# Fifteen instead of nine paired projection parts in the first block, the convolution's four among them

## The chip, the cores and the metric

The kernel runs on one NeuronCore of one Trainium2 chip. TensorE multiplies matrices, VectorE (DVE) and ScalarE (ACT) work element by element, GpSimd (POOL) does little here, and SyncE (SP) issues the DMAs. The metric is the device time of one launch in microseconds: 2176.01 us, the median of three runs (2175.82 to 2176.3).

## The reference, cut to what matters

Two transformer blocks of two layers each follow one another, on 256 rows of 1024 values. The change touches only the first block, whose mixer begins with one wide projection. Its parts go to a state-space branch with a short convolution, and to three kinds of attention:

```python
def causal_dwconv(u, w, b):
    width = w.shape[0]                                    # 4 taps
    up = jnp.pad(u, ((0, 0), (width - 1, 0), (0, 0)))
    y = lax.conv_general_dilated(up, w[:, None, :], window_strides=(1,), padding='VALID',
                                 dimension_numbers=('NWC', 'WIO', 'NWC'),
                                 feature_group_count=u.shape[-1])
    return y + b

def hybrid_mixer(h, w_in, ...):
    u = h @ w_in                                          # [256, 1024] @ [1024, D_IN]
    (z, xs, bs, cs, dt_raw, fq, fk, fv, ff, mq, mk, mv, dq, dk, dv, iq, ik, iw) = jnp.split(
        u, np.cumsum(IN_SPLITS)[:-1].tolist(), axis=-1)
    y_ssm = mamba2_branch(z, xs, bs, cs, dt_raw, ...)      # silu(causal_dwconv(xs, bs, cs)), then a scan
    y_fox = fox_branch(fq, fk, fv, ff, fox_fbias)
    ...
```

The result must agree with float32 arithmetic, so every product is made of split operands: a weight w becomes whi + wlo and an activation x becomes nhi + nlo, and three products (whi nhi, whi nlo, wlo nhi) are summed.

## The kernel before

**Parts.** The weights come in parts of 1 MB, numbered h in the order in which TensorE wants them. Parts 0 to 3 are the lead (z and fv). Part 4 holds a few narrow columns. Parts 5 to 8 hold the 1024 channels of the convolution (256 channels each, two blocks of 128), part 9 the index queries, parts 10 and 11 fq, parts 12 and 13 fk, then the rest. For each part SyncE issues a DMA, ScalarE makes the high half (`hi`, L1161), VectorE the low half (`lo`, L1444), and TensorE multiplies.

**Two ways to multiply a part of 256 channels.** A plain part fills one PSUM bank: its block m = 0 goes to columns 0 to 255 and m = 1 to 256 to 511. `block_of` (L656) issues three matmuls of 256 columns for each of eight row blocks k, so 24 for a block of 128 channels. A paired part (list `PAIRED`) fills a bank for each block of 128 channels: `apart_block` multiplies whi once with nlo and nhi side by side (512 columns, L666, 8 matmuls), then wlo with nhi (256 columns, L670, 8 matmuls). The bank then holds two sums in two halves. ScalarE copies one to SBUF (`evict_half`, L1202) and VectorE adds the other to it (`add_half`, L1695).

**Banks.** Units of the projection alternate between banks 0 and 1. `bank(key)` makes TensorE wait until the unit two before has been freed:

```python
            u = unit[key]
            if u >= 2:
                pe.wait_ge(*freed[u - 2])
```

A plain unit is a whole part and is freed by ScalarE's copy (`free_a`). A paired unit is a half part and is freed by VectorE's addition (`pair_sum`).

**The order on each engine is written by hand,** one step i after another. VectorE in step i does: the addition of half 1 of part i-1, `lo(i + 2)`, the addition of half 0 of part i, and then what belongs to the step. That is two blocks of the convolution each in steps 6 to 9, the small softplus chain in 6 and 9 (`softplus_1` to `softplus_3`, L1536 to L1563), `cumulated` in 11, the rotations `rope(0)` and `rope(1)` in 12, and `state_inputs` in 13 (L1602, L1604). One block b of the convolution is one L1518 and three L1521, each waiting for the one before it. ScalarE in step i does: the copy of part i-1 (or of its half 1), `hi(i + 3)`, the copy of half 0 of part i, and then its own extras. In step 9 an `Ln` waits for VectorE's `softplus_2`, and in step 10 come two `Silu`, the first of which (L1325) waits for the whole convolution.

**Between the parts TensorE does** `cumulate` after part 10 (L830, L833), `state_scores` in the middle of part 12 (L841 to L847, ends with `xs_ps`), and `decay(0)` after two matmuls of part 14 (L857 and on). The last waits for `xs_ok`, which `state_inputs` gives.

SyncE swaps halves of the index queries for the rotation once part 9 has been freed.

Of the kernel before, what the change touches and what calls it, by code (L numbers as in the profile page):

```python
# [132 lines left out]
def earlier(n_first, n_second):  # L133
# [6 lines left out]
GAINED_1 = {  # L140
    "wk_ps": 18, "wk_free": 9, "qv_ps": 9,
    "gpost_in": 64, "par_in": 48, "small_in": 96, "sgw_in": 320,
    "w_small": 368, "tr_ps": 8, "full": 51, "half_used": 44, "par_ps": 1, "few_ps": 1, "cum_ps": 5, "cb_ps": 1,
    "xs_ps": 1, "dec_ps": 8, "ix_ps": 1, "y_ps": 1, "qk_ps": 12, "yt_ps": 4, "pt_ps": 6, "o_ps": 6, "pr_ps": 16,
    "out_used": 3, "mix_ps": 2, "dn_ps": 2, "in_ms": 4, "hi_ok": 87, "nhi_ok": 8, "free_a": 33, "spe": 21,
    "silu_ok": 2, "cb_ok": 1, "dec_ok": 8, "ix_rl": 1, "ex_ok": 12, "yt_out": 1, "pt_a": 6, "ot_ok": 6,
    "sig_ok": 4, "yh_ok": 4, "mh_ok": 4, "ssq_ok": 6, "ms_ok": 6, "fg_free": 11, "hh_ok": 11, "xn_ok": 8,
    "nlo_ok": 8, "lo_ok": 87, "pad_ok": 2, "par_ok": 1, "spv": 20, "lcat_ok": 5, "cum_ok": 2, "free_v": 10,
    "rope_ok": 10, "xs_ok": 1, "sc_ok": 2, "msq_ok": 1, "mx_ok": 12, "yt_ok": 1, "pn_ok": 12, "pt_v": 6,
    "isc_ok": 1, "pen_ok": 2, "yl_ok": 4, "pr_free": 16, "mg_ok": 14, "ml_ok": 4, "x_ok": 4, "fu_free": 11,  # L150
    "hs_ok": 11, "in_rs": 2, "rstd_ok": 7
}
GAINED_2 = {
# [51 lines left out]
FEW = [(0, 6416, 68), (68, 1516, 28), (96, 3056, 32)]  # L205
H_FEW, H_XBC = 4, 5
ROWS_1 = (19, 24)
PAIRED = (10, 11, 13, 14, 15, 16, 21, 22, 23)
C_IW, C_DT, C_FF = 64, 88, 120
N_GATE1 = 16  # L210
N_PARTS1 = N_IN1 + N_GATE1 + 12 + HID1 // 128 + KH1 // 2
# [26 lines left out]
def first_block(nc, ctx, sems, n_chain, ps, x, x_in, con, con_in, con_bf, bfc, start, a):  # L238
# [107 lines left out]
    hi_ok, lo_ok = sem("hi_ok"), sem("lo_ok")  # L346
    full, free_a, free_v = (sem(n) for n in ("full", "free_a", "free_v"))
    par_ps, par_ok = sem("par_ps"), sem("par_ok")
    ssq_ok, ms_ok, msq_ok, rstd_ok = sem("ssq_ok"), sem("ms_ok"), sem("msq_ok"), sem("rstd_ok")
# [7 lines left out]
    in_ms, in_rs = sem("in_ms"), sem("in_rs")  # L357
# [8 lines left out]
    fg_free, fu_free, hh_ok, hs_ok, dn_ps = (sem(n) for n in ("fg_free", "fu_free", "hh_ok", "hs_ok", "dn_ps"))  # L366
    sum_a, gate_sum, up_sum = sem("wk_ps"), sem("wk_free"), sem("qv_ps")
    dch = sem("dch")
    pair_half, pair_sum = spe, spv
    bias_in, biased, mg_turned = [small_in, swap_in[1]], lcat_ok, cum_ps  # L370
    BIAS_BEFORE = (64, 336)

# [47 lines left out]
    order = []  # L420
    order += [("lead", name, t) for _, name in LEAD for t in range(NT)]
    for i in range(4, N_IN1 + N_GATE1):
        order += [("in", i, n) for n in range(2 if i in PAIRED else 1)] if i < N_IN1 else [("gate", i - N_IN1)]
    unit = {key: u for u, key in enumerate(order)}
    pairs = {("in", i, n): 2 * PAIRED.index(i) + n + 1 for i in PAIRED for n in range(2)}
    freed = [(pair_sum, 2 + pairs[key]) if key in pairs else (free_a, n + 1 - sum(k in pairs for k in order[:n]))
             for n, key in enumerate(order)]
    filled = {key: n + 1 for n, key in enumerate(order)}

# [207 lines left out]
    def tensor(pe, l, prior, following):  # L637
# [384 lines left out]
        for n in range(4):  # L1022
            yhi, ylo = ybuf[n % 2]
            for m in range(4):
                h, t = H_BR + 2 * n + m // 2, m % 2
                i = 4 * n + m
                if m == 0:
                    pe.wait_ge(yl_ok, n + 1)
                if t == 0:
                    pe.wait_ge(lo_ok, h + 1)  # L1030
                if i == 15:
                    merged_turn(0)
                if i >= 4:
                    pe.wait_ge(pr_free, i - 3)
                hi, lo = high(l, h), low(l, h)
                for k in range(4):
                    for j, (x_, w) in enumerate(((ylo, hi), (yhi, lo), (yhi, hi))):
                        mm = T.matmul(ps[:, 4 + i % 4, :], x_[:, k, t * P:(t + 1) * P], w[:, k, :],  # L1038
                                      start=k == 0 and j == 0, stop=k == 3 and j == 2)
                mm.then_inc(pr_ps, 1)  # L1040
# [122 lines left out]
    def scalar(act, l, prior, following):  # L1163
# [133 lines left out]
        for i in range(1, H_BR):  # L1297
            if i <= 2:
                evict_lead(i - 1)
            if i == 4:  # L1300
                evict_lead(2)
                evict_lead(3)
            if i == 5:
                act.wait_ge(par_ok, 1)
            if 5 <= i <= N_IN1:
                if i - 1 == 22:
                    act.wait_ge(qk_ps, 4)
                if i - 1 in PAIRED:
                    evict_half(i - 1, 1)
                elif i - 1 not in ROWS_1:  # L1310
                    evict(i - 1)
            hi(i + 3)
            if i in PAIRED:
                if i == 22:
                    act.wait_ge(qk_ps, 4)
                evict_half(i, 0)
            if i > N_IN1:
                evict_gate(i - 1 - N_IN1)
            if i - 1 in ROWS_1:
                if i - 1 == ROWS_1[1]:  # L1320
                    act.wait_ge(o_ps, 2)
                evict(i - 1)
            if i == 10:
                act.wait_ge(pad_ok, 2)
                S.activation(xbc[:, :, :], xbc[:, :, :], ACT.Silu).then_inc(silu_ok, 1)  # L1325
                act.wait_ge(*freed[unit["lead", "z", 1]])
                S.activation(z[:, :, :], z[:, :, :], ACT.Silu).then_inc(silu_ok, 1)
            if i == 8:
                act.wait_ge(spv, 1)
                S.activation(sp[:, 2, :], sp[:, 1, :], ACT.Exp, scale=-1.0).then_inc(spe, 1)  # L1330
                act.wait_ge(small_in, 64)
                S.activation(asg[:, 0:8], small[:, 1, :], ACT.Exp).then_inc(spe, 1)
            if i == 9:
                act.wait_ge(spv, 2)
                S.activation(sp[:, 4, :], sp[:, 3, :], ACT.Ln).then_inc(spe, 1)
            if i == 13:
                act.wait_ge(cb_ps, 1)
                S.copy(cb[:, :, :], ps[:, 2:4, 0:384]).then_inc(cb_ok, 1)
            if i == 14:
                decays(0)  # L1340
            if i == 15:
                decays(1)
            if i == 17:
                relus()
            if i == 20:
                y_out()
            for n in range(6):
                if i == Q_STEP[n]:
                    exps(n, 0)
                if i == Q_STEP[n] + 1:  # L1350
                    exps(n, 1)
                if i == Q_STEP[n] + 2:
                    p_out(n)
                if i == Q_STEP[n] + 4:
                    o_out(n)
            if i == 37:
                branch_hi(0)
                sigmoids(0)
            if i == 38:
                branch_hi(1)  # L1360
            if i == 39:
                sigmoids(1)
            if i == 41:
                sigmoids(2)
# [113 lines left out]
    def vector(dve, l, prior, following):  # L1478
# [33 lines left out]

        def convolve(b):
            if b % 2 == 0:
                dve.wait_ge(*freed[unit["in", H_XBC + b // 2, 0]])
            dve.wait_ge(pad_ok, 1)
            dve.wait_ge(par_ok, 1)
            link(V.tensor_scalar(xbc[:, b, :], xbcp[:, b, 0:SEQ], parT[:, PCW + b:PCW + b + 1],  # L1518
                                 parT[:, PCB + b:PCB + b + 1], ALU.mult, ALU.add))
            for j in range(1, 4):  # L1520
                ins = V.scalar_tensor_tensor(xbc[:, b, :], xbcp[:, b, j:j + SEQ],  # L1521
                                             parT[:, PCW + 8 * j + b:PCW + 8 * j + b + 1],
                                             xbc[:, b, :], ALU.mult, ALU.add)
                if b == 7 and j == 3:
                    ins.then_inc(pad_ok, 1)
                else:
                    link(ins)
# [163 lines left out]
        def add_half(i, m):  # L1691
            _, _, _, name, at_ = IN1[i][2][0]
            out = dst[name][:, at_ + m, :]
            dve.wait_ge(pair_half, 3 + pairs["in", i, m])
            V.scalar_tensor_tensor(out, ps[:, unit["in", i, m] % 2, SEQ:2 * SEQ], QSCALE.get(name, 1.0), out,  # L1695
                                   ALU.mult, ALU.add).then_inc(pair_sum, 1)

# [6 lines left out]
        def gated(i):  # L1704
            n, m = i // 4, i % 4
            if m == 0:
                dve.wait_ge(sig_ok, n + 1)
            dve.wait_ge(pr_ps, i + 1)
            src = ps[:, 4 + i % 4, :]
            t, c = m % 2, 512 * (m // 2)  # L1710
            gt = gates_of(n)[:, t, c:c + 512]
            out = merged[:, t, c:c + 512]
            product = rt[:, :, :].rearrange("p a b -> p (a b)")
            if n == 0:
                V.tensor_tensor(out, src, gt, ALU.mult).then_inc(pr_free, 1)
                return
            if i > 4:
                dve.wait_ge(mg_ok, i - 4)
            V.tensor_tensor(product, src, gt, ALU.mult).then_inc(pr_free, 1)
            dve.wait_ge(pr_free, i + 1)  # L1720
            V.tensor_tensor(out, out, product, ALU.add).then_inc(mg_ok, 1)
# [2487 lines left out]
```

## Time and profile before

| | us |
|---|---|
| median of three runs | 2176.01 |
| the profiled execution | 2175.88 |
| its span, first to last instruction | 2174.0 |
| TensorE busy | 2157.4 (99%) |
| VectorE busy | 1487.8 (68%) |
| ScalarE busy | 1118.6 (51%) |

The span is cut into instructions for each engine. A row of the timeline has the start, the time to the end, the engine, the line, output and inputs, and in brackets how long the engine had been idle and who released it. Matmuls overlap, so the time that one costs is read from start to start. In the same way a VectorE instruction's successor starts some 0.08 us before its end. The first block's first layer has its projection from about 21 us on; the second layer repeats it 532.1 us later.

### The profile page before, as it was taken

To read this page: it belongs to the slowest core of one execution; us is meant where nothing else is said; L and a number is where in the kernel's file an instruction comes from. 1 tells how busy PE (TensorE), PEld (TensorE's weight loads), DVE (VectorE), ACT (ScalarE), POOL (GpSimd) and SP (SyncE) were. 2 spreads that over 40 slices of the span, in tenths; PEclk is the share of its full clock that TensorE was granted. 3 is DMA by queue.
4 is the path that set the end of the run, shared out by engine and by line. 5 is a ranking of instruction groups with operands and counts; after the bars stand their busy time and mean duration, and the time that the engine had idled before them with its cause. 6 is when DMAs were issued, how large, how long until landed. Compare 5 with 4: busy or idle time off the path is not lost.

```text
span 2174.0 us, 30972 instructions
## 1 busy us (share of the span) xinstructions
PE 2157.4 (99%) x13072; PEld 1852.7 (85%) x13072; DVE 1487.8 (68%) x1660; ACT 1118.6 (51%) x1413; POOL 44.7 (2%) x46
## 2 busy tenths in 40 slices
PE   8999999999999999999999999999999999999998
PEld 7988888888988888888898888988889888898887
DVE  6788677655778868666678777456557877745654
ACT  5555555454565564545466535444446653544442
POOL 0000000000000000000000100000000010000000
PEclk9999999999999999999999999999999999999999
DMA  8555564655664556556564444456566444545652
GB/s 278 167 167 176 168 232 160 208 197 168 198 186 155 162 204 203 177 190 214 161 197 135 143 150 162 150 170 192 191 171 204 134 143 151 160 151 169 193 192 76
DMA packets 248751, 380.75 MB, mean 175 GB/s; under 512 B 22495, under 2 KB 158693, under 8 KB 248614
## 3 DMA queue, kind: packets, MB, share of 16 engines
q1 hardware_dynamic: 248614, 378.78, 54.2%
q8 instruction: 103, 1.69, 0.3%
q14 instruction: 34, 0.28, 0.0%
HBM read 372.26 MB, written 1.05 MB: 172 GB/s over the span
## 4 chain that ended last, share of the span: by engine, by line
PE 97%; DVE 2%; ACT 1%; issue 1%; DMA 0%; POOL 0%; DVEq 0%; SPq 0%; POOLq 0%; ACTq 0%
PE ps L666 9%; PE ps L2567 8%; PE ps L803 8%; PE ps L3137 8%; PE ps L2471 7%; PE ps L2518 5%; PE ps L1135 5%; PE ps L2492 5%; PE ps L670 5%; PE ps L656 5%; PE ps L2625 4%; PE ps L1038 4%; PE ps L2494 2%; PE ps L762 2%; PE ps L1056 2%; PE ps L2588 2%
## 5 line engine op out<-in xcount | busy, mean ns | idle before, releaser
L3498 DVE TENSOR_TENSOR b_wlo<-b_ring,b_whi 128x2048 fp32r<-128x2048 f32 (+2 forms) x168 | 379.4, 2262 | 107.8 <-ACT b_whi L3162 107.1
L1444 DVE TENSOR_TENSOR a_wlo<-a_ring,a_whi 128x2048 fp32r<-128x2048 f32 (+1 forms) x173 | 392.8, 2273 | 56.9 <-ACT a_whi L1161 56.5
L3162 ACT CAST b_whi<-b_ring 128x2048 fp32r<-128x2048 f32 (+2 forms) x168 | 318.1, 1893 | 202.2 <-PE ps L3137 76.0
L1161 ACT CAST a_whi<-a_ring 128x2048 fp32r<-128x2048 f32 (+1 forms) x173 | 329.0, 1903 | 150.1 <-PE ps L1038 45.2
L666 PE MATMUL ps<-a_nsp,a_whi 128*128 128x512 f32 x864 | 218.4, 394 | 0.0
L666 PEld LDWEIGHTS ps<-a_nsp,a_whi 128*128 128x128 f32 x864 | 155.2, 189 | 27.9
L2567 PE MATMUL ps<-b_whi,b_nsp 128*128 128x512 f32 x512 | 170.9, 400 | 0.0
L803 PE MATMUL ps<-a_whi,a_nsp 128*128 128x512 f32 x512 | 162.3, 392 | 0.0
L670 PEld LDWEIGHTS ps<-a_nsp,a_wlo 128*128 128x128 f32 x864 | 117.8, 190 | 8.5
L670 PE MATMUL ps<-a_nsp,a_wlo 128*128 128x256 f32 x864 | 120.4, 282 | 0.0
L2567 PEld LDWEIGHTS ps<-b_whi,b_nsp 128*128 128x128 f32 x512 | 96.1, 188 | 20.9
L803 PEld LDWEIGHTS ps<-a_whi,a_nsp 128*128 128x128 f32 x512 | 96.1, 188 | 20.3 <-issue 0.3
L2492 PE MATMUL ps<-b_nsp,b_whi 128*128 128x512 f32 x448 | 112.5, 393 | 0.0
L2567 PE MATMUL ps<-b_wlo,b_nsp 128*128 128x512 f32 x256 | 99.9, 390 | 0.0
L3137 PE MATMUL ps<-b_whi,b_hlo 128*128 128x512 f32 x256 | 99.8, 390 | 0.0
L803 PE MATMUL ps<-a_wlo,a_nsp 128*128 128x512 f32 x256 | 99.7, 389 | 0.0
L3137 PE MATMUL ps<-b_wlo,b_hhi 128*128 128x512 f32 x256 | 99.6, 389 | 0.0
L3137 PE MATMUL ps<-b_whi,b_hhi 128*128 128x512 f32 x256 | 99.6, 389 | 0.0
L2471 PE MATMUL ps<-b_nsp,b_whi 128*128 128x256 f32 x544 | 98.5, 283 | 0.0
L656 PE MATMUL ps<-a_nsp,a_whi 128*128 128x256 f32 x544 | 98.4, 283 | 0.0
L2492 PEld LDWEIGHTS ps<-b_nsp,b_whi 128*128 128x128 f32 x448 | 80.6, 189 | 14.5
L2471 PEld LDWEIGHTS ps<-b_nsp,b_whi 128*128 128x128 f32 x544 | 84.8, 192 | 0.1
(614 smaller groups left out, 4426.2 us busy)
## 6 DMA issues: line engine op xcount, KB each, us to landing
a_ring<-in_w_in SPq DMA_DIRECT2D x49, 1024.0 KB, 5.4
b_ring<-in_w_in SPq DMA_DIRECT2D x46, 1024.0 KB, 5.1
a_ring<-in_w_ffn_in SPq DMA_DIRECT2D x44, 1024.0 KB, 5.1
a_ring<-in_w_gate SPq DMA_DIRECT2D x32, 1024.0 KB, 5.4
b_ring<-in_w_up SPq DMA_DIRECT2D x32, 1024.0 KB, 5.5
b_ring<-in_w_down SPq DMA_DIRECT2D x32, 1024.0 KB, 4.9
a_ring<-in_w_ffn_out SPq DMA_DIRECT2D x22, 1024.0 KB, 5.0
a_ring<-in_w_branch SPq DMA_DIRECT2D x16, 1024.0 KB, 5.1
```

The source lines that it names most:

```text
L656: mm = T.matmul(out, w[:, k, c:c + P], x_[:, k, :], start=k == 0 and n == 0, stop=k == KD - 1 and n == 2)
L666: T.matmul(ps[:, bank_, :], hi[:, k, c:c + P], nsp[:, k, :], start=k == 0, stop=False)
L670: mm = T.matmul(ps[:, bank_, 0:SEQ], lo[:, k, c:c + P], nhi[:, k, :], start=False, stop=k == KD - 1)
L803: mm = T.matmul(ps[:, GATE_BANK[j % 3], :], x_[:, k, t * P:(t + 1) * P], w[:, kk, :], start=k == 0 and n == 0, stop=k == KD - 1 and n == 2)
L1161: nc.scalar.copy(high(l, h), raw(l, h)).then_inc(hi_ok, 1)
L1444: nc.vector.tensor_tensor(low(l, h), raw(l, h), high(l, h).bitcast(F32), ALU.subtract).then_inc(lo_ok, 1)
L2471: mm = T.matmul(out, w[:, k, c:c + P], x_[:, k, :], start=k == 0 and n == 0, stop=k == KD - 1 and n == 2)
L2492: T.matmul(ps[:, bank_, :], hi[:, k, c:c + P], nsp[:, k, :], start=k == 0, stop=False)
L2567: mm = T.matmul(b, x_[:, k, t * P:(t + 1) * P], w[:, kk, :], start=k == 0 and j == 0, stop=k == KD - 1 and j == 2)
L3137: mm = T.matmul(ps[:, 4 + 2 * t + half, :], hidden_of(x_, i)[:, kk, t * P:(t + 1) * P], w[:, kk, half * 512:(half + 1) * 512], start=i + k ...
L3162: nc.scalar.copy(high(l, h), raw(l, h)).then_inc(hi_ok, 1)
L3498: nc.vector.tensor_tensor(low(l, h), raw(l, h), high(l, h).bitcast(F32), ALU.subtract).then_inc(lo_ok, 1)
```

## The change

Parts 5 to 9 and 12 join the list of paired parts. Their products are made by `apart_block`, ScalarE copies them in halves, and VectorE adds the other halves. The counters for halves copied and halves added move to semaphores that count from zero. A copy of the first half of part 12 waits until TensorE has read what lies in its place (`xs_ps`). The convolution waits for the second half of its part.

```diff
@@ counts of events per layer @@
-    "w_small": 368, "tr_ps": 8, "full": 51, ...
+    "w_small": 368, "tr_ps": 8, "full": 57, ...
...
-PAIRED = (10, 11, 13, 14, 15, 16, 21, 22, 23)
+PAIRED = (5, 6, 7, 8, 9, 10, 11, 12, 13, 14, 15, 16, 21, 22, 23)
+N_PAIRS = 2 * len(PAIRED)
...
-    pair_half, pair_sum = spe, spv
+    pair_half, pair_sum = sig_ok, yl_ok
...
-    freed = [(pair_sum, 2 + pairs[key]) if key in pairs else (free_a, n + 1 - sum(k in pairs for k in order[:n]))
+    freed = [(pair_sum, pairs[key]) if key in pairs else (free_a, n + 1 - sum(k in pairs for k in order[:n]))
...
-                    pe.wait_ge(yl_ok, n + 1)
+                    pe.wait_ge(yl_ok, N_PAIRS + n + 1)
...
             if i in PAIRED:
+                if i == 12:
+                    act.wait_ge(xs_ps, 1)
                 if i == 22:
                     act.wait_ge(qk_ps, 4)
                 evict_half(i, 0)
...
         def convolve(b):
             if b % 2 == 0:
-                dve.wait_ge(*freed[unit["in", H_XBC + b // 2, 0]])
+                dve.wait_ge(*freed[unit["in", H_XBC + b // 2, 1 if H_XBC + b // 2 in PAIRED else 0]])
...
-            dve.wait_ge(pair_half, 3 + pairs["in", i, m])
+            dve.wait_ge(pair_half, pairs["in", i, m])
...
-                dve.wait_ge(sig_ok, n + 1)
+                dve.wait_ge(sig_ok, N_PAIRS + n + 1)
```

What stands in VectorE's queue around step 7 of the first layer, from the end of step 6 to the first tap of step 8, before. `a_wlo` is the low half of a part's weights, `a_xbcp` the input of the convolution and `a_xbc` its output, `a_sp` belongs to the softplus chain:

```order
L1543 SCALAR_TENSOR_TENSOR a_sp<-a_sp 128x32 [waits dch]
L1444 TENSOR_TENSOR a_wlo<-a_ring,a_whi 128x2048 [waits hi_ok]
L1518 TENSOR_SCALAR a_xbc<-a_xbcp,a_parT 128x256 [waits par_ok,pad_ok,free_a]
L1521 SCALAR_TENSOR_TENSOR a_xbc<-a_xbcp,a_parT,a_xbc 128x256 [waits dch] x3
L1518 TENSOR_SCALAR a_xbc<-a_xbcp,a_parT 128x256 [waits par_ok,pad_ok,dch]
L1521 SCALAR_TENSOR_TENSOR a_xbc<-a_xbcp,a_parT,a_xbc 128x256 [waits dch] x3
L1444 TENSOR_TENSOR a_wlo<-a_ring,a_whi 128x2048 [waits hi_ok,dch]
L1518 TENSOR_SCALAR a_xbc<-a_xbcp,a_parT 128x256 [waits par_ok,pad_ok,free_a]
```

And now, where lines are three higher, `sig_ok` counts ScalarE's halves and `yl_ok` VectorE's sums:

```order
L1546 SCALAR_TENSOR_TENSOR a_sp<-a_sp 128x32 [waits dch]
L1698 SCALAR_TENSOR_TENSOR a_xbcp<-ps,a_xbcp 128x256 [waits sig_ok]
L1447 TENSOR_TENSOR a_wlo<-a_ring,a_whi 128x2048 [waits hi_ok]
L1698 SCALAR_TENSOR_TENSOR a_xbcp<-ps,a_xbcp 128x256 [waits sig_ok]
L1521 TENSOR_SCALAR a_xbc<-a_xbcp,a_parT 128x256 [waits par_ok,pad_ok,yl_ok]
L1524 SCALAR_TENSOR_TENSOR a_xbc<-a_xbcp,a_parT,a_xbc 128x256 [waits dch] x3
L1521 TENSOR_SCALAR a_xbc<-a_xbcp,a_parT 128x256 [waits par_ok,pad_ok,dch]
L1524 SCALAR_TENSOR_TENSOR a_xbc<-a_xbcp,a_parT,a_xbc 128x256 [waits dch] x3
L1698 SCALAR_TENSOR_TENSOR a_xbcp<-ps,a_xbcp 128x256 [waits sig_ok,dch]
L1447 TENSOR_TENSOR a_wlo<-a_ring,a_whi 128x2048 [waits hi_ok]
```

Two additions stand in the step, one on each side of the low half of the weights. The second addition of a part stands behind all eight instructions of the step's convolution.

ScalarE's queue around part 12, before (`a_whi` is the high half of the weights, `a_cb` the scores of `state_scores`):

```order
L1161 CAST a_whi<-a_ring 128x2048 [waits landed1,full]
L1193 ACTIVATE a_fk<-ps 128x512 [waits full]
L1161 CAST a_whi<-a_ring 128x2048 [waits landed2,full]
L1202 ACTIVATE a_fk<-ps 128x256 [waits full]
L1338 COPY a_cb<-ps 128x768 [waits cb_ps]
```

And now:

```order
L1162 CAST a_whi<-a_ring 128x2048 [waits landed1,full]
L1203 ACTIVATE a_fk<-ps 128x256 [waits full,xs_ps]
L1203 ACTIVATE a_fk<-ps 128x256 [waits full]
L1162 CAST a_whi<-a_ring 128x2048 [waits landed2,full]
L1203 ACTIVATE a_fk<-ps 128x256 [waits full]
L1341 COPY a_cb<-ps 128x768 [waits cb_ps]
```

The one copy of part 12 has become two, and the first waits for `xs_ps`.

## Rows read from the trace of the kernel before

**Rows 1.** The page: busy time of the engines, with shares of the span and instructions.

```profile
PE 2157.4 (99%) x13072; PEld 1852.7 (85%) x13072; DVE 1487.8 (68%) x1660; ACT 1118.6 (51%) x1413; POOL 44.7 (2%) x46
```

**Rows 2.** TensorE's waits, 0 to 700 us: in total, times, longest.

```profile
PE ps L1009 <- DMA con<-in_constants: 4.8, 1, 4.8
PE ps L698 <- DVE a_nsp L625: 1.7, 2, 1.0
...
```

**Rows 3.** Timeline of TensorE: part 5, the start of 6, and parts 10 and 11.

```profile
40.89 0.28 PE L656 MATMUL ps<-a_nsp,a_wlo 128*128 128x256 f32 x1
...
46.65 0.38 PE L824 MATMUL ps<-con,a_iqf 128*128 128x128 f32 x2
46.79 0.36 PE L656 MATMUL ps<-a_nsp,a_wlo 128*128 128x256 f32 x1
...
72.70 2.00 PE L666 MATMUL ps<-a_nsp,a_whi 128*128 128x512 f32 x8
...
75.49 1.02 PE L830 MATMUL ps<-con,a_lcat 128*128 128x256 f32 x4
...
76.94 2.10 PE L666 MATMUL ps<-a_nsp,a_whi 128*128 128x512 f32 x8
```

**Rows 4.** Timeline of VectorE, steps 6 to 8.

```profile
51.51 0.17 DVE L1536 TENSOR_SCALAR a_iw<-ps 128x8 f32<-128x8 f32 x1
...
52.19 2.29 DVE L1444 TENSOR_TENSOR a_wlo<-a_ring,a_whi 128x2048 fp32r<-128x2048 f32 x1
54.39 0.41 DVE L1518 TENSOR_SCALAR a_xbc<-a_xbcp,a_parT 128x256 f32<-128x256 f32 x1
...
58.41 2.29 DVE L1444 TENSOR_TENSOR a_wlo<-a_ring,a_whi 128x2048 fp32r<-128x2048 f32 x1
```

**Rows 5.** Timeline of VectorE, steps 9 to 12.

```profile
66.85 0.41 DVE L1518 TENSOR_SCALAR a_xbc<-a_xbcp,a_parT 128x256 f32<-128x256 f32 x1
...
70.74 0.18 DVE L1548 TENSOR_SCALAR a_sp<-a_sp 128x32 f32<-128x32 f32 x1
...
73.29 2.28 DVE L1444 TENSOR_TENSOR a_wlo<-a_ring,a_whi 128x2048 fp32r<-128x2048 f32 x1
...
83.23 0.42 DVE L1695 SCALAR_TENSOR_TENSOR a_fq<-ps,a_fq 128x256 f32<-128x256 f32 x1 [0.63 <-ACT a_fq L1202]
83.57 2.28 DVE L1444 TENSOR_TENSOR a_wlo<-a_ring,a_whi 128x2048 fp32r<-128x2048 f32 x1
```

**Rows 6.** Timeline of ScalarE, steps 10 to 12.

```profile
73.76 1.28 ACT L1325 ACT_TABLE_LOAD   x1
...
77.82 0.36 ACT L1202 ACTIVATE a_fq<-ps 128x256 f32<-128x256 f32 x1
...
82.81 0.38 ACT L1202 ACTIVATE a_fq<-ps 128x256 f32<-128x256 f32 x1 [2.41 <-PE ps L670]
```

**Rows 7.** Timeline of VectorE, steps 12 and 13.

```profile
85.77 0.69 DVE L1574 TENSOR_TENSOR a_rt<-a_swap,a_con 128x512 f32<-128x512 f32 x1
...
89.98 2.29 DVE L1444 TENSOR_TENSOR a_wlo<-a_ring,a_whi 128x2048 fp32r<-128x2048 f32 x1
...
94.30 0.68 DVE L1602 TENSOR_TENSOR a_xd<-ps,a_sp 128x512 f32<-128x512 f32 x1
```

**Rows 8.** Timeline of TensorE: second half of part 12, and decay(0).

```profile
87.59 0.36 PE L656 MATMUL ps<-a_nsp,a_wlo 128*128 128x256 f32 x1
...
96.83 0.50 PE L857 MATMUL ps<-a_cumS,a_sel 64*128 64x256 f32 x4
```

**Rows 9.** Timeline of TensorE, the second layer's part 10, half 1.

```profile
604.80 2.00 PE L666 MATMUL ps<-a_nsp,a_whi 128*128 128x512 f32 x8
```

**Rows 10.** Timeline of TensorE near the start.

```profile
12.28 1.05 PE L698 MATMUL ps<-a_whi,a_nsp 128*128 128x512 f32 x2
13.14 0.63 PE L698 MATMUL ps<-a_wlo,a_nsp 128*128 128x512 f32 x1
```

**Rows 11.** Windows: length, busy PE, PEld, DVE, ACT, POOL, granted clock, DMA share, GB/s.

```profile
12.00:14.00 2.00, 2.00 (x7) 1.52 (x6) 1.25 (x2) 2.00 (x3) 0.00 (x0) 1.00 1.06 404
```

More of the change, by code:

```diff
@@ L142 @@
     "gpost_in": 64, "par_in": 48, "small_in": 96, "sgw_in": 320,
-    "w_small": 368, "tr_ps": 8, "full": 51, "half_used": 44, "par_ps": 1, "few_ps": 1, "cum_ps": 5, "cb_ps": 1,
+    "w_small": 368, "tr_ps": 8, "full": 57, "half_used": 44, "par_ps": 1, "few_ps": 1, "cum_ps": 5, "cb_ps": 1,
     "xs_ps": 1, "dec_ps": 8, "ix_ps": 1, "y_ps": 1, "qk_ps": 12, "yt_ps": 4, "pt_ps": 6, "o_ps": 6, "pr_ps": 16,
-    "out_used": 3, "mix_ps": 2, "dn_ps": 2, "in_ms": 4, "hi_ok": 87, "nhi_ok": 8, "free_a": 33, "spe": 21,
+    "out_used": 3, "mix_ps": 2, "dn_ps": 2, "in_ms": 4, "hi_ok": 87, "nhi_ok": 8, "free_a": 27, "spe": 3,
     "silu_ok": 2, "cb_ok": 1, "dec_ok": 8, "ix_rl": 1, "ex_ok": 12, "yt_out": 1, "pt_a": 6, "ot_ok": 6,
-    "sig_ok": 4, "yh_ok": 4, "mh_ok": 4, "ssq_ok": 6, "ms_ok": 6, "fg_free": 11, "hh_ok": 11, "xn_ok": 8,
-    "nlo_ok": 8, "lo_ok": 87, "pad_ok": 2, "par_ok": 1, "spv": 20, "lcat_ok": 5, "cum_ok": 2, "free_v": 10,
+    "sig_ok": 34, "yh_ok": 4, "mh_ok": 4, "ssq_ok": 6, "ms_ok": 6, "fg_free": 11, "hh_ok": 11, "xn_ok": 8,
+    "nlo_ok": 8, "lo_ok": 87, "pad_ok": 2, "par_ok": 1, "spv": 2, "lcat_ok": 5, "cum_ok": 2, "free_v": 10,
     "rope_ok": 10, "xs_ok": 1, "sc_ok": 2, "msq_ok": 1, "mx_ok": 12, "yt_ok": 1, "pn_ok": 12, "pt_v": 6,
-    "isc_ok": 1, "pen_ok": 2, "yl_ok": 4, "pr_free": 16, "mg_ok": 14, "ml_ok": 4, "x_ok": 4, "fu_free": 11,
+    "isc_ok": 1, "pen_ok": 2, "yl_ok": 34, "pr_free": 16, "mg_ok": 14, "ml_ok": 4, "x_ok": 4, "fu_free": 11,
     "hs_ok": 11, "in_rs": 2, "rstd_ok": 7
```

## The prediction

> **What bounds the kernel now.** I read the busy times first. TensorE works 99% of the span [rows 1], so its queue is the clock of the kernel, and other engines matter only where it waits for them. Its waits come next. In the first 700 us, which hold both places of the change, the only large ones are at the very start, 4.8 us for a DMA and 1.7 us in two pieces [rows 2]. So in the projection nobody keeps TensorE waiting. I then read TensorE's timeline from start to start for what a part costs, and at last VectorE's timeline in the same stretch. There the reader is to see that VectorE has no slack in the convolution: one step, from one low half of weights to the next, lasts 58.41 - 52.19 = 6.22 us [rows 4], while TensorE's part lasts 46.65 - 40.89 = 5.76 us [rows 3]. VectorE falls behind there, and nothing shows of it, since TensorE needs nothing of the convolution until the middle of part 12.
>
> **What the change removes.** A plain block of 128 channels is 24 matmuls at 0.12 us (48 in 5.76 us), so 2.88 us. A paired one runs from 72.70 to 75.49, 2.79 us [rows 3]. That saves 0.09 us a half, on 6 parts x 2 halves x 2 layers = 24 halves: 2.2 us. It lies wholly on the path and is all that the change can give.
>
> **What it adds.** Six more copies on ScalarE and twelve more additions on VectorE in each layer. An addition is 0.42 us and its successor starts 0.34 us after it [rows 5]. It starts 0.42 us after ScalarE's copy, which starts 0.20 us after TensorE's half has ended (82.81 for a half that ended at 76.94 + 2.88 + 2.79 = 82.61, then 83.23) [rows 3, 5, 6]. Four operations of `state_inputs` need 3 x 0.60 + 0.68 = 2.48 us, and TensorE starts 2.53 us after the first [rows 7, 8], so I take 0.06 us for the release and 0.48 us from an addition's start to the matmul that it frees.
>
> More weighs what the additions now hold. Before, a plain unit was a whole part, and TensorE could take a bank two parts later. Now each bank is one half, the next half in the same bank comes 2.79 us after, and it is freed by VectorE. The addition of half 1 of part i stands in VectorE's queue behind the convolution of step i. So TensorE's half 1 of part i+1 waits for it: VectorE's lag, hidden before, becomes TensorE's.
>
> **First layer, steps 5 to 10.** VectorE's pieces, from start to start: a low half 54.39 - 52.19 = 2.20, two convolution blocks 58.41 - 54.39 = 4.02, softplus_1 0.68 [rows 4]; the last two blocks 3.89 and softplus_2 and _3 2.55 (66.85, 70.74, 73.29) [rows 5].
> Part 5 starts at 40.89 and now ends at 46.47. After the short transpose of 0.14 us and 0.08 us that its first matmul is longer (0.36 for 0.28 us) [rows 3], half 0 of part 6 starts at 46.69 and ends at 49.48. Its addition starts at 49.48 + 0.62 = 50.10. From there VectorE never idles:
> - rest of step 6: 0.34 + 4.02 + 0.68 = 5.04
> - steps 7 and 8, each 0.34 + 2.20 + 0.34 + 4.02 = 6.90
> - step 9: 0.34 + 2.20 + 0.34 + 3.89 + 2.55 = 9.32
>
> In sum 28.16 us, so the addition of half 1 of part 9 starts at 78.26 and frees TensorE at 78.74. TensorE left to itself would be there at 46.69 + 9 x 2.79 = 71.80. The 6.94 us between come as four waits, each for the addition behind a convolution: before half 1 of part 7 the addition starts at 55.14, TensorE comes at 55.06 and goes at 55.62 (0.56); before half 1 of part 8 62.04 gives 62.52 for 61.20 (1.32); before part 9's 68.94 gives 69.42 for 68.10 (1.32); before part 10's 78.74 for 75.00 (3.74). Half 1 of part 10 started at 72.70 before [rows 3], so the shift is **6.04 us**; ten cheaper halves are already in it.
>
> **Steps 10 to 14.** Half 1 of part 10 ends at 81.53. `cumulate` takes 76.94 - 75.49 = 1.45, part 11 takes 2.88 + 2.79, half 0 of part 12 takes 2.79: 91.44. `state_scores` takes 87.59 - (82.61 + 2.88) = 2.10 us [rows 3, 8], to 93.54. Here the new wait for `xs_ps` bites. ScalarE may copy half 0 of part 12 only then, and VectorE's addition of it starts at 94.16. Queued behind it are both rotations (89.98 - 85.77 = 4.21 us) [rows 7], to 98.71, the addition of half 1 of part 12, the low half of part 15 and the addition of half 0 of part 13 (0.34 + 2.20 + 0.34), so `state_inputs` starts at 101.59 and lets `decay(0)` go at 104.12. TensorE would come there at 93.54 + 0.10 + 3 x 2.79 + 2 x 0.23 = 102.5, and waits 1.6 us. `decay(0)` started at 96.83 before [rows 8]. Shift here: **7.3 us**. Half 1 of part 13 wants its bank at 99.2, and the addition behind the rotations frees it at 99.2, so nothing more is lost there.
>
> ScalarE is never last in this: in step 10 its two Silu with their table load take 77.82 - 73.76 = 4.06 us [rows 6] and end near 82.6, and the half copied behind them is wanted by TensorE only at 85.9. The swap of the index queries waits for part 9 until 78.7 and is wanted at 94.5. After `decay(0)` every engine stands as before, later by the same 7.3 us, and since TensorE had no idle time from there on, nothing gives it back.
>
> **The sum.** The second layer's half 1 of part 10 stands at 604.80, 532.10 us after the first's [rows 3, 9], and its queues are the same, so it pays the same. 2 x 7.3 = 14.6 us. Against the profiled execution of 2175.88 us that is 2190.5; the median of the runs is 0.13 us higher, so I say **2190.6 us**. Bounds for one layer: if an addition on `a_xbcp` costs its full 0.42 us in the queue, nine of them on the chain add 0.7 us and each wake of TensorE may cost 0.2 us more: 8.4 us. If VectorE's pieces pack 0.1 us better at each of the twelve joints, 6.1 us. So 2188 to 2192.8.
>
> **Rivals.**
> - *VectorE keeps up* and only the 2.2 us of saving shows: 2173.8 us. It is not slower than before. The mechanism is that a half's bank is free when TensorE comes. It decides at half 1 of part 10: the 28.16 us of VectorE's work between 50.10 and the release would have to fit into 71.80 - 0.48 - 50.10 = 21.2 us. For it speaks that VectorE is busy only 68% in all [rows 1]. Against it, that four steps of 6.22 us are already longer than TensorE's, before anything is added. 4%.
> - *The delay is partly absorbed*: only the four waits at the additions behind the convolution count, and `state_inputs` is in time, as it would be if the rotations or the softplus chain overlapped more. Then the shift is 5 to 6 us a layer less up to 1 us for shorter waits, 2 x 4.5 = 9, about 2185. Rows speak against it, since every piece waits for its forerunner on one engine. 9%.
> - *TensorE comes back slow from the wait of 3.7 us.* Near the start, after its 4.8 us of idling, two matmuls of 512 columns took 13.14 - 12.28 = 0.86 us, 0.43 each, which is 1.2 GHz, where a paired one takes 0.23 us, which is 2.4 GHz [rows 3, 10]; the granted clock is given as 1.00 for that stretch nevertheless [rows 11]. If half 1 of part 10 and cumulate ran so, they would take some 4.2 us more, of which nothing is hidden, or 2 us for half of it: 2194 to 2199. Against it: the wait is shorter than the one at the start. 9%. The Trainium skill, "TensorE: Matmul & The Clock Gate", section "HAM oscillation — how this bites in real kernels", says that idle gaps of a few microseconds make the engine start at half clock again. By that rule this rival would be the likeliest case; the rows before the change have no such gap in the projection and neither bear it out nor refute it.
> - The forecast, 78%.
>
> **The numbers.** A measurement of this kernel can tell about 0.2%, 4.4 us, from no change. The first rival is within that. All others lie above 2180.4. So slower 0.95, same 0.04, faster 0.01. The range takes the forecast's bounds, half of the absorbed case and the lower end of the slow clock: 2186 to 2195.
>
> **What would show it.** In the trace after: TensorE idle before L667 (the first matmul of a half) for VectorE's L1698 on `a_xbcp` and `a_iqf`, four times a layer, 0.6, 1.3, 1.3 and 3.7 us, and once for `a_xd`, 1.6 us; VectorE without a gap from about 50 to 78 us; the halves of parts 5 to 9 at 2.79 us; `decay(0)` near 104.1 and 96.83 + 532.10 + 14.6 = 643.5 us. If TensorE shows no waits there, the step that is wrong is that of the bank. If the waits are there and the time isn't, something later gave it back. If L667 is spaced 0.43 us after the longest wait, the clock rival holds.

## The result, and the profile after

The changed kernel takes 2194.65 us (median of five runs, 2192.41 to 2195.17) against 2176.01 us before (five runs too, 2175.82 to 2176.3). The ratio is 1.0084, with a 95% interval of 1.0073 to 1.0094. That is 18.6 us slower; 14.6 us were forecast, and the range of 2186 to 2195 holds it. The profiled execution took 2194.65 us with a span of 2192.6 us.

The page's busy times [rows 1] now read:

```profile
PE 2162.5 (99%) x12880; PEld 1846.9 (84%) x12880; DVE 1496.0 (68%) x1684; ACT 1120.9 (51%) x1425; POOL 44.7 (2%) x46
```

TensorE has 192 matmuls fewer and is still busy 5.1 us longer, and 13.5 us more of its span are idle time. The busy share, 99% as before, shows nothing of either. The waits show it. This is the view of TensorE's waits from 0 to 720 us (in total, times, longest), where the one large one before was that of the start [rows 2]:

```profile
PE ps L667 <- DVE a_iqf L1698: 6.9, 2, 3.5
PE ps L667 <- DVE a_xbcp L1698: 4.9, 6, 1.0
PE ps L1010 <- DMA con<-in_constants: 4.6, 1, 4.6
PE ps L858 <- DVE a_xd L1607: 2.8, 2, 1.4
...
```

L1698 is the addition, L667 the first matmul of a half, L858 belongs to `decay(0)`. Without the DMA's, these are ten waits, five a layer, 14.6 us in all, and it is these that the prediction listed. TensorE's timeline around the longest wait (start, time to the end, and in brackets the idle time before and its releaser) answers to [rows 3]:

```profile
62.28 2.11 PE L667 MATMUL ps<-a_nsp,a_whi 128*128 128x512 f32 x8 [1.03 <-DVE a_xbcp L1698]
...
65.18 2.00 PE L667 MATMUL ps<-a_nsp,a_whi 128*128 128x512 f32 x8
...
69.16 2.12 PE L667 MATMUL ps<-a_nsp,a_whi 128*128 128x512 f32 x8 [1.03 <-DVE a_xbcp L1698]
...
78.47 3.78 PE L667 MATMUL ps<-a_nsp,a_whi 128*128 128x512 f32 x8 [3.44 <-DVE a_iqf L1698]
82.05 1.91 PE L671 MATMUL ps<-a_nsp,a_wlo 128*128 128x256 f32 x8
83.75 1.24 PE L831 MATMUL ps<-con,a_lcat 128*128 128x256 f32 x4
...
106.62 0.50 PE L858 MATMUL ps<-a_cumS,a_sel 64*128 64x256 f32 x4 [1.39 <-DVE a_xd L1607]
```

The reader is to see two things. First, the waits fall where they were forecast. Second, the half at 78.47 lasts to 83.75, 5.28 us where a half lasts 2.79 us, or 2.90 behind a short wait. The second layer has the same: it waits 3.45 us, begins at 620.61, and ends at 624.83 after 4.22 us. The granted clock says why. Windows of the changed kernel, first layer and second (length, busy PE, PEld, DVE, ACT, POOL, granted clock, DMA share, GB/s):

```profile
76.00:77.00 1.00, 0.00 (x0) 0.00 (x0) 0.90 (x4) 1.00 (x2) 0.00 (x0) 1.00 0.03 8
77.00:78.00 1.00, 0.00 (x0) 0.00 (x0) 0.90 (x9) 1.00 (x2) 0.00 (x0) 0.68 0.00 0
78.00:79.00 1.00, 0.53 (x1) 0.50 (x2) 1.00 (x3) 0.98 (x2) 0.00 (x0) 0.50 0.00 0
...
84.00:85.00 1.00, 1.00 (x7) 0.83 (x6) 0.59 (x2) 1.00 (x2) 0.00 (x0) 0.91 0.15 34
...
619.00:620.00 1.00, 0.00 (x0) 0.00 (x0) 0.90 (x7) 1.00 (x2) 0.00 (x0) 1.00 0.00 0
620.00:621.00 1.00, 0.39 (x1) 0.39 (x2) 1.00 (x5) 0.98 (x3) 0.00 (x0) 0.54 0.00 0
...
623.00:624.00 1.00, 1.00 (x6) 0.81 (x4) 0.09 (x1) 1.00 (x2) 0.00 (x0) 0.75 0.52 127
```

A clock of 1.00 is 2.4 GHz, and 0.50 is 1.2 GHz. In the first layer TensorE goes idle at 75.03 (78.47 - 3.44). Windows of 0.1 us put the fall of the clock at 77.4, still inside the wait, and its rise at 84.2. In the second layer it goes idle at 617.16, the clock falls at 620.1 and rises at 623.5. So matmuls ran at half rate for 5.7 us in the first layer (78.47 to 84.2) and for 2.9 us in the second (620.61 to 623.5). Half of each, 2.9 and 1.4 us, is my estimate of what that cost.

VectorE's timeline shows what TensorE waits for. The same stretch as [rows 4, 5], steps 7 to 10:

```profile
54.92 0.42 DVE L1698 SCALAR_TENSOR_TENSOR a_xbcp<-ps,a_xbcp 128x256 f32<-128x256 f32 x1
...
61.80 0.42 DVE L1698 SCALAR_TENSOR_TENSOR a_xbcp<-ps,a_xbcp 128x256 f32<-128x256 f32 x1
...
68.69 0.42 DVE L1698 SCALAR_TENSOR_TENSOR a_xbcp<-ps,a_xbcp 128x256 f32<-128x256 f32 x1
...
75.46 0.17 DVE L1551 TENSOR_SCALAR a_sp<-a_sp 128x32 f32<-128x32 f32 x1
...
77.99 0.42 DVE L1698 SCALAR_TENSOR_TENSOR a_iqf<-ps,a_iqf 128x256 f32<-128x256 f32 x1
```

The steps are 6.88 and 6.89 us long (6.90 forecast), where TensorE needs 5.58. The addition of half 1 of part 9 stands behind the softplus chain and starts at 77.99. This execution began its projection 0.22 us earlier than the one before (part 4 at 37.70, not 37.92), so the forecast's 78.26 would be 78.04 here, and is off by 0.05 us. VectorE's only gap between 50 and 78 us is 0.37 us, for ScalarE's logarithm inside the chain; the kernel before has the same gap (0.37 us, at 71.29).

To compare layers I use one measure from here on: the time from the start of part 4 to `decay(0)`, and from there to the second layer's `decay(0)`. Before they are 96.83 - 37.92 = 58.91 and 628.93 - 96.83 = 532.10 us. In the changed kernel they are 68.92 and 540.87, so the shift is 10.01 us in the first layer and 8.77 in the second, 18.8 in sum, against 18.6 in time. So nothing to speak of is lost elsewhere.

### The profile page after: what moved, and what is told of

Same layout as the page of the kernel before. It is cut to its first block, busy times and chain, and to the rows that moved or that the text cites. A ratio compares the mean times of both kernels' runs of the same rounds, so it can differ in the third digit from the quotient of the medians.

```text
span 2192.6 us, 30626 instructions
## 1 busy us (share of the span) xinstructions
PE 2162.5 (99%) x12880; PEld 1846.9 (84%) x12880; DVE 1496.0 (68%) x1684; ACT 1120.9 (51%) x1425; POOL 44.7 (2%) x46
## 4 chain that ended last, share of the span: by engine, by line
PE 94%; DVE 4%; issue 1%; ACT 1%; DMA 0%; POOL 0%; DVEq 0%; SPq 0%; POOLq 0%; ACTq 0%
PE ps L667 9%; PE ps L2570 8%; PE ps L804 8%; PE ps L3140 8%; PE ps L2474 7%; PE ps L2521 5%; PE ps L1136 5%; PE ps L671 5%; PE ps L2495 5%; PE ps L2628 4%; PE ps L1039 4%; PE ps L2497 2%; PE ps L763 2%; PE ps L1057 2%; PE ps L699 2%; PE ps L2591 2%
## 5 line engine op out<-in xcount | busy, mean ns | idle before, releaser
L667 PE MATMUL ps<-a_nsp,a_whi 128*128 128x512 f32 x1056 | 270.8, 398 | 11.8 <-DVE a_iqf L1698 6.9
L667 PEld LDWEIGHTS ps<-a_nsp,a_whi 128*128 128x128 f32 x1056 | 191.6, 191 | 48.3 <-DVE a_iqf L1698 7.3
L2570 PE MATMUL ps<-b_whi,b_nsp 128*128 128x512 f32 x512 | 170.9, 400 | 0.0
L671 PEld LDWEIGHTS ps<-a_nsp,a_wlo 128*128 128x128 f32 x1056 | 144.9, 191 | 10.6
L671 PE MATMUL ps<-a_nsp,a_wlo 128*128 128x256 f32 x1056 | 147.9, 283 | 0.0
L2628 PE MATMUL ps<-b_whi,b_nsp 128*128 128x512 f32 x256 | 82.6, 395 | 0.7 <-DVE b_nsp L3868 0.7
```

The lines of the kernel that those rows point to most:

```text
L667: T.matmul(ps[:, bank_, :], hi[:, k, c:c + P], nsp[:, k, :], start=k == 0, stop=False)
L671: mm = T.matmul(ps[:, bank_, 0:SEQ], lo[:, k, c:c + P], nhi[:, k, :], start=False, stop=k == KD - 1)
L2570: mm = T.matmul(b, x_[:, k, t * P:(t + 1) * P], w[:, kk, :], start=k == 0 and j == 0, stop=k == KD - 1 and j == 2)
L2628: mm = T.matmul(ps[:, OUT_BANK[t] + half, :], x_[:, k, t * P:(t + 1) * P], w[:, kk, half * 512:(half + 1) * 512], start=k == 0 and j == 0, ...
```

## The experiments

Seven kernels ran, each compared with the kernel before on the same chip (2175.96 us for the first four, 2175.85 for the other three).

**1. TensorE kept busy during its longest wait.**

```diff
+                    if (i, m) == (10, 1):
+                        for _ in range(14):
+                            T.matmul(ps[:, 6, :], high(l, i)[:, 0, 0:P], nsp[:, 0, :], start=True, stop=True)
                     bank(("in", i, m))
```

> The changed kernel, and in front of half 1 of part 10, where TensorE waits some 3.4 us for VectorE, 14 spare matmuls of 512 columns into a bank that nobody reads then (14 x 0.23 = 3.2 us, less than the wait). Theory A: after that wait TensorE ran at half rate (half 1 of part 10 took 5.28 and 4.22 us instead of 2.79, cumulate 1.67 instead of 1.45 us), because it had been idle. With the wait filled, the same half takes 2.79 us in both layers and the time is 2194.65 - 2.71 - 1.43 = 2190.5 us, nearly what the waits alone make. Rival B: the half is slow for another reason (contention with what VectorE, ScalarE or the DMAs do at that time); then nothing changes and it stays near 2194.6, or gets longer if the spare matmuls delay it.

Measured: 2190.85 us (2190.68 to 2190.99), ratio 1.0068 (1.0055 to 1.0081). TensorE's timeline in the first layer:

```profile
75.09 3.36 PE L781 MATMUL ps<-a_nsp,a_whi 128*128 128x512 f32 x14
78.70 2.14 PE L667 MATMUL ps<-a_nsp,a_whi 128*128 128x512 f32 x8 [0.25 <-DVE a_iqf L1701]
80.67 1.10 PE L671 MATMUL ps<-a_nsp,a_wlo 128*128 128x256 f32 x8
```

The half starts as late as before the experiment (0.23 us later by the clock of the trace, as this execution's projection began), yet its eight wide matmuls take 2.14 instead of 3.78 us, and the granted clock is 1.00 in every window from 74 to 86 us and from 615 to 626 us. The shift is 7.46 us in each layer. Work that is thrown away makes the kernel 3.8 us faster, so theory A holds and rival B falls: 10.01 - 7.46 = 2.6 us in the first and 8.77 - 7.46 = 1.3 us in the second layer were the slow clock. The rest, 14.9 us, is what the waits cost, less the saving. It also narrows the runs: 0.3 us between the lowest and the highest, where the changed kernel has 2.8.

**2. Part 9's second half copied and added ahead of the softplus chain,** and no longer at its old place.

```diff
             if i == 9:
+                evict_half(9, 1)
                 act.wait_ge(spv, 2)
...
             if i == 9:
+                add_half(9, 1)
                 softplus_2()
```

> The changed kernel, with ScalarE's copy and VectorE's addition of half 1 of part 9 ahead of the softplus chain instead of behind it; nothing else moves. Theory A (waits at the bank, set by the place of the addition in VectorE's queue): the addition starts near 75.5 instead of 78.0, the wait of 3.4 us shrinks to about 1.0, TensorE does not go slow behind it, and the shift at decay(0) is 3.5 + 1.2 = 4.7 us a layer: 2185.4 us. Rival C (it is VectorE's sum of work that counts, wherever the addition stands: TensorE then waits as long for the softplus result at cumulate): 2190.5 or more.

Measured: 2187.44 us (2187.05 to 2187.62), ratio 1.0052 (1.0039 to 1.0066). TensorE's timeline:

```profile
75.82 2.12 PE L667 MATMUL ps<-a_nsp,a_whi 128*128 128x512 f32 x8 [0.91 <-DVE a_iqf L1700]
...
78.73 1.02 PE L831 MATMUL ps<-con,a_lcat 128*128 128x256 f32 x4
...
80.99 2.08 PE L667 MATMUL ps<-a_nsp,a_whi 128*128 128x512 f32 x8 [0.66 <-DVE a_fq L1700]
```

The wait of 3.4 us is now 0.9 us, the clock stays up, and `cumulate` (L831) follows at once; rival C's wait for the softplus result isn't there. The shift is 5.7 us in each layer, where 4.7 were expected. I missed the time by 2.0 us, since I hadn't worked out the next addition. VectorE's timeline has it:

```profile
77.81 0.50 DVE L1568 TENSOR_TENSOR a_lcat<-a_sp,a_asg 128x32 f32<-128x32 f32 x4
78.22 2.28 DVE L1449 TENSOR_TENSOR a_wlo<-a_ring,a_whi 128x2048 fp32r<-128x2048 f32 x1
80.43 0.42 DVE L1700 SCALAR_TENSOR_TENSOR a_fq<-ps,a_fq 128x256 f32<-128x256 f32 x1
```

The addition of half 0 of part 10 stands behind the softplus chain and a low half of weights. In the changed kernel TensorE was so late that this cost nothing. With one wait gone, the next in VectorE's queue shows.

**3. Only the convolution's parts paired.**

```diff
-PAIRED = (5, 6, 7, 8, 9, 10, 11, 12, 13, 14, 15, 16, 21, 22, 23)
+PAIRED = (5, 6, 7, 8, 10, 11, 13, 14, 15, 16, 21, 22, 23)
```

> Only the convolution's parts 5 to 8 are added to the old list, parts 9 and 12 stay plain. Theory A: three short waits become two or so (0.4 and 1.0 us) and one before half 1 of part 10, which now waits for ScalarE's copy of part 9, held behind the logarithm and so behind VectorE's convolution: 2.4 us. The shift is 3.6 us a layer, 2183.1 us in all, and TensorE stays at full rate after the 2.4 us. Rival D (the loss comes from part 9 and part 12, not from the convolution): about 2175 us.

Measured: 2184.18 us (2183.95 to 2186.55), ratio 1.004 (1.0026 to 1.0054). The waits of TensorE, 0 to 720 us:

```profile
PE ps L667 <- ACT a_iqf L1194: 4.4, 2, 2.2
PE ps L667 <- DVE a_xbcp L1698: 2.8, 4, 1.0
```

The shift is 3.7 us in each layer (3.6 forecast); the time is 1.1 us above. Here the longest wait comes by way of ScalarE: its copy of part 9 (L1194) stands behind a logarithm (L1338), and that one waits for VectorE's L1551, behind the last two blocks of the convolution. ScalarE's timeline:

```profile
75.71 0.23 ACT L1338 ACTIVATE a_sp<-a_sp 128x32 f32<-128x32 f32 x1 [6.47 <-DVE a_sp L1551]
75.85 0.58 ACT L1194 ACTIVATE a_iqf<-ps 128x512 f32<-128x512 f32 x1
```

Rival D falls: pairing the convolution's parts alone costs 8 us. After the 2.2 us of idling the half takes 2.90 us with its start, full rate. That holds for the profiled execution, which took 2183.96 us. Of the other three, two took 2183.95 and 2184.39 us at the same mean granted clock, 0.999. The fourth took 2186.55 us at 0.997. It has no trace, but 2.6 us more at a lower clock is what one slow stretch can cost in the changed kernel. So 2.2 us of idling may not always be harmless.

**4. Only parts 5 and 12 paired.** The number of newly paired parts has to be even here, so that later units keep their banks; part 5 costs nothing when VectorE does the low half of part 8 first.

```diff
-PAIRED = (5, 6, 7, 8, 9, 10, 11, 12, 13, 14, 15, 16, 21, 22, 23)
+PAIRED = (5, 10, 11, 12, 13, 14, 15, 16, 21, 22, 23)
...
+            if i == 6:
+                lo(i + 2)
             if i - 1 in PAIRED:
                 add_half(i - 1, 1)
-            lo(i + 2)
+            if i != 6:
+                lo(i + 2)
```

> Only parts 5 and 12 are added to the old list, and in step 6 VectorE makes the low half of part 8 before the addition of part 5, so that part 5 costs nothing. Theory A: the wait for xs_ps at part 12 pushes the rotations and with them state_inputs back, so decay(0) starts 1.07 us later a layer, with the 0.36 us saved already in it: 2178.1 us. Rival E (part 12 is harmless, and its term of 1.6 us in the prediction came only on top of VectorE's lag): 2176.0 - 0.7 = 2175.3 us.

Measured: 2178.31 us (2177.98 to 2178.79), ratio 1.0011 (1.0002 to 1.002). TensorE waits for nothing in the projection but this:

```profile
97.76 0.50 PE L858 MATMUL ps<-a_cumS,a_sel 64*128 64x256 f32 x4 [1.39 <-DVE a_xd L1607]
```

The shift is 1.15 us a layer (1.07 forecast). The wait of `decay(0)` is there without any wait in the convolution, so it needs no lag of VectorE from before.

**5. The same with both rotations behind `state_inputs`.**

```diff
-ROPE = [("iqk", 0, 2, 9, 16, 12), ("iqk", 2, 1, 4, 16, 12), ...
+ROPE = [("iqk", 0, 2, 9, 16, 14), ("iqk", 2, 1, 4, 16, 14), ...
```

> The last kernel (parts 5 and 12 added), with the two rotations of the index queries moved in VectorE's queue from step 12 to step 14, behind state_inputs. Theory A: the addition of part 12 is no longer followed by 4.2 us of rotations before state_inputs, decay(0) waits for nothing, and 4 halves of 0.09 us and the 0.14 us that decay(0) waited before are gained in each layer: 2176.0 - 1.0 = 2175.0 us. Rival E (the wait for xs_ps itself costs the time): it stays at 2178.3.

Measured: 2175.75 us (2175.29 to 2176.13), ratio 0.9999 (0.999 to 1.0008). The 1.15 us of part 12 are gone, by moving 4.2 us of work that nobody needed there, and the wait for `xs_ps` is still in the kernel; rival E falls. Of the 1.0 us that I wanted beyond, the time shows 0.1, within what can be told, and the two stretches 0.33 and 0.18. Part of it I had booked wrongly: `decay(0)` still starts 0.70 us after half 0 of part 14, as before. `state_inputs` stands behind the addition of half 0 of part 13, whose half TensorE ends at 93.16, and 0.62 + 0.34 + 2.53 us later is 96.65, where `decay(0)` starts.

**6. Four parts, 5, 6, 9 and 12, with the pieces moved.** Beside the edits of experiments 2, 4 and 5, and with the low half of part 9 moved ahead in step 7 as that of part 8 is in step 6:

```diff
+PAIRED = (5, 6, 9, 10, 11, 12, 13, 14, 15, 16, 21, 22, 23)
...
             if i == 6:
+                add_half(6, 0)
                 softplus_1()
```

> Parts 5, 6, 9 and 12 are added to the old list, with the rotations in step 14, the low halves of parts 8 and 9 ahead of the additions in steps 6 and 7, the addition of half 0 of part 6 behind the convolution of step 6, and the copy and addition of half 1 of part 9 ahead of the softplus chain. Theory A: no wait of TensorE in the projection, 8 halves of 0.09 and 0.14 us gained a layer: 2176.0 - 1.7 = 2174.3 us. Rival C (VectorE's added work of 2.7 us a layer must show somewhere): 2176 or more.

Measured: 2177.13 us (2176.76 to 2177.59), ratio 1.0006 (0.9997 to 1.0015). I missed by 2.8 us. The addition of part 10 behind the softplus chain is late here too:

```profile
74.96 1.02 PE L831 MATMUL ps<-con,a_lcat 128*128 128x256 f32 x4
75.82 0.74 PE L834 MATMUL ps<-a_lcat,con 128*128 128x16 f32 x6
77.22 2.06 PE L667 MATMUL ps<-a_nsp,a_whi 128*128 128x512 f32 x8 [0.66 <-DVE a_fq L1700]
```

Before, half 0 of part 11 followed the row of `cumulate`'s second line after 0.6 us; here it takes 1.4. It is the same wait as in experiment 2, and the expectation had overlooked it in both. The time alone lies where rival C put it, at 2176 or more; only the next experiment decides between the two.

**7. All fifteen parts, the same instructions in another order.** VectorE's steps 6 to 13 are written out. The start of them, here with a step's calls on one line:

```diff
+            if i == 6:
+                lo(8); add_half(5, 1); convolve(0); softplus_1(); add_half(6, 0); convolve(1)
+            if i == 7:
+                add_half(6, 1); lo(9); add_half(7, 0); convolve(2); convolve(3)
+            if i == 8:
+                add_half(7, 1); convolve(4); add_half(8, 0); lo(10)
+            if i == 9:
+                add_half(8, 1); convolve(5); add_half(9, 0); convolve(6)
+            if i == 10:
+                add_half(9, 1); lo(11); add_half(10, 0); softplus_2(); convolve(7); softplus_3()
...
+            if i == 13:
+                add_half(12, 0); state_inputs(); add_half(12, 1); lo(15); add_half(13, 0)
```

The rotations, `cumulate` and some of ScalarE's copies move too.

> All fifteen parts paired as in the changed kernel, with the same instructions in another order. VectorE in steps 6 to 13: an addition stands between any two convolution blocks where one falls due, low halves of weights come later, softplus_2 and _3 around the last block; the rotations in step 14; cumulate after part 11 instead of 10; ScalarE copies the halves of parts 9, 10 and 11 as soon as they are full. Theory A (the loss is one of order, since TensorE waits for a bank only as long as its addition stands behind other work): no wait, 12 halves of 0.09 and 0.14 us gained a layer: 2176.0 - 2.4 = 2173.6 us, up to 1 us more where an addition falls a tenth or two late. Rival C (VectorE's sum of work is too long for the stretch): waits of 1 us or more a layer stay, 2178 or more.

Measured: 2174.13 us (2173.65 to 2174.43) beside 2175.85 (2175.62 to 2177.22), ratio 0.9991 (0.9982 to 1.0). All its runs lie below all runs of the kernel before, though the interval touches 1. TensorE has no wait in either layer's projection. Its timeline:

```profile
69.42 2.00 PE L667 MATMUL ps<-a_nsp,a_whi 128*128 128x512 f32 x8
...
72.21 2.00 PE L667 MATMUL ps<-a_nsp,a_whi 128*128 128x512 f32 x8
...
75.00 2.00 PE L667 MATMUL ps<-a_nsp,a_whi 128*128 128x512 f32 x8
```

The halves follow at 2.79 us right through the softplus chain. VectorE did no less: the page has its busy time and instructions as in the changed kernel (1496.0 us, x1684).

```profile
PE 2156.5 (99%) x12880; PEld 1843.4 (85%) x12880; DVE 1496.5 (69%) x1684; ACT 1121.2 (52%) x1425; POOL 44.7 (2%) x46
```

Its timeline shows the other order, with an addition on either side of the low half:

```profile
70.11 0.42 DVE L1704 SCALAR_TENSOR_TENSOR a_iqf<-ps,a_iqf 128x256 f32<-128x256 f32 x1
70.45 2.28 DVE L1453 TENSOR_TENSOR a_wlo<-a_ring,a_whi 128x2048 fp32r<-128x2048 f32 x1
72.83 0.43 DVE L1704 SCALAR_TENSOR_TENSOR a_fq<-ps,a_fq 128x256 f32<-128x256 f32 x1
...
77.12 0.42 DVE L1704 SCALAR_TENSOR_TENSOR a_fq<-ps,a_fq 128x256 f32<-128x256 f32 x1
```

In the first layer the stretch is 1.16 us shorter than before (1.22 forecast), in the second 0.85, so 2.0 us are there of the 2.4 expected (2.2 of pairing and twice 0.14 before `decay(0)`). Rival C falls: it wasn't VectorE's sum of work but the order of the work. The gain in time is 1.7 us; this execution began its projection 0.38 us later, which no experiment traces.

## Why the prediction was right, and where it was short

- **The saving** of 0.09 us a half was right: halves of the new parts are 2.79 us apart (experiment 7).
- **The bank as the place of the wait**, and the addition behind the convolution as its cause, were right. The four waits were forecast at 0.56, 1.32, 1.32 and 3.74 us; the rows give 0.38, 1.03, 1.03 and 3.44 us of idling. Idle time counts from the modelled end of the last matmul; read from start to start, as the forecast was, the waits are 0.54, 1.19, 1.19 and 3.61 us. Each wake also makes the half 0.11 us longer (62.28 to 65.18 is 2.90 us), which the forecast had left out. Half 1 of part 10 starts 5.99 us late against 6.04 forecast. Experiment 7 shows the cause: the same instructions in another order, and no wait.
- **Part 12 and the rotations** were forecast at some 1.6 us of waiting and measured at 1.39 us of idling (1.56 from start to start), in the changed kernel as in experiment 4 by themselves. Experiment 5 shows that the rotations make it.
- **The shift without the clock**, 7.3 us a layer, was measured at 7.46 us (experiment 1), which is 2190.85 us where I said 2190.6.
- **The clock** is the term that was missing from the likeliest case. It stood among the rivals at 9%, at 4.2 us a layer for the whole of half 1 of part 10 and `cumulate`, or 2 us for half of it. Experiment 1 takes away 2.6 and 1.3 us, 3.8 us in time. The step that failed is the reason given against it, "the wait is shorter than the one at the start". That the longest idle time known is longer says nothing of how short one is still too long. By the rule of the Trainium skill's "TensorE: Matmul & The Clock Gate", section "HAM oscillation — how this bites in real kernels", which I had cited and outweighed, this was the likeliest case. The trace agrees with it: a granted clock of 0.50 behind 3.44 us of idling.
- **The range** holds the time in part by luck. The forecast's own bounds ended at 2192.8 us, and four of the five runs lie above that. The range went on to 2195 only for the low end of the rival given 9%, and one run, at 2195.17, lies outside even so. Had the second layer paid the first one's 2.6 us, the time would have been near 2196.
- In the expectation of experiment 5 I booked 0.14 us before `decay(0)` as a wait that goes. The experiment shows that it stays, as long as `state_inputs` follows the addition of part 13.

What stays open: how short an idle time of TensorE is harmless here. The clock fell 2.3 us after TensorE went idle in the first layer and 2.9 us after in the second, idling of 2.2 us kept full rate in the one traced execution of experiment 3, and an untraced one may have lost it. The prices of 2.6 and 1.3 us follow from how long matmuls then ran at half rate, 5.7 and 2.9 us; why that differs between the layers no run shows. The runs of the changed kernel, spread over 2.8 us with granted clocks of 0.997 to 0.999, would fit a price that differs from run to run; that is argued, not shown.

## What to carry to other kernels

When a buffer's release moves from one engine to another, read the new engine's queue at every place of use: what stands ahead of the releasing instruction is what the other engine will wait for, however little the instruction itself costs. An engine that falls behind without harm (6.22 us a step beside 5.76 here) is using slack that the next edit may take, and interleaving the same instructions by their due times gave 20 us back. Add to any new wait of TensorE of some microseconds the price of the matmuls behind it at half rate, here 1.3 to 2.6 us each time.

## What the runs showed of the hardware

TensorE idled 3.4 us, and the next half ran its 512-column matmuls at nearly twice their time: 3.78 us instead of 2.00 for eight, with a granted clock of 0.50 in the windows. The clock had fallen before TensorE woke, 2.3 us into the idle time in one layer and 2.9 us in the other. Idling of 1.0 and 2.2 us did nothing of the kind in the profiled executions. Fourteen matmuls of no use, 3.36 us long, put in the wait kept it at full rate and saved 3.8 us. At the start of the kernel a spacing of 0.43 us for 512-column matmuls, twice the 0.23 us of full rate, stands under a granted clock of 1.00 [rows 10, 11], so there the spacing of equal matmuls tells more than the clock column.
